# Two transformer blocks on one core: transposes placed inside matmul groups, the projection of p in four pieces, and six slabs of the second input projection by seven block products

## The reference, cut to what matters

```python
# first block, after both mixers
merged = sigmoid(ga) * (y_a @ w_branch_a) + sigmoid(gb) * (y_b @ w_branch_b)
h = h + rms_norm(merged @ w_out, norm_post_mix)
v = rms_norm(h, norm_pre_mlp)
h = h + rms_norm(square(relu(v @ w_up)) @ w_down, norm_post_mlp)
e = (p @ w_ple) * sigmoid(h @ w_ple_gate)      # p: 256 x 256
h = h + rms_norm(e, norm_ple)
# second block
qa, ka, va, qb, kb, vb, qi, ki, wi, ga, gb = split(rms_norm(h, g_mix_2) @ w_in_2)
# rope on qa, ka, qb, kb, qi, ki; two attentions; 32 experts of three matrices each
```

## Time and profile before

| | us |
|---|---|
| median of 3 runs | 1460.21 (1456.59 to 1465.51) |
| the profiled execution's own time | 1465.0 |
| its span, first to last instruction | 1463.2 |
| TensorE busy | 1217.1 (83%) |
| VectorE, ScalarE, GpSimd busy | 396.3, 233.0, 137.6 |
| mean granted TensorE clock | 0.922 of full speed |

### The profile page before, as it was taken

One profiled execution on the slowest core, in us unless ns is written; L12 is line 12 of the kernel. 1 busy time (PEld: TensorE's weight loads), 2 busy tenths in 40 slices (PEclk: granted clock), 3 DMA queues, 4 the chain that ended last, 5 costly groups with the idle time before them and its releaser, 6 DMA issues.

```text
span 1463.2 us, 13835 instructions
## 1 busy us (share of the span) xinstructions
PE 1217.1 (83%) x5929; PEld 687.9 (47%) x5929; DVE 396.3 (27%) x734; ACT 233.0 (16%) x455; POOL 137.6 (9%) x165
## 2 busy tenths in 40 slices
PE   7999999999998999999899999887564664656545
PEld 7846655556844998444444446444221221212211
DVE  2242333035514553644322352213000000000002
ACT  1130003126601221000200165001000000000001
POOL 1001003000210223631112000100000000000000
PEclk9999999999999999999999999997887887868868
DMA  9532222431134344343334210692999999999994
GB/s 370 218 123 112 79 106 110 165 145 58 58 137 153 150 173 173 137 179 157 117 115 173 87 58 29 274 384 110 429 428 429 427 427 428 429 427 427 428 424 186
DMA packets 26980, 330.66 MB, mean 226 GB/s; under 512 B 4112, under 2 KB 4896, under 8 KB 6176
## 3 DMA queue, kind: packets, MB, share of 16 engines
q1 hardware_dynamic: 26912, 329.70, 56.0%
HBM read 328.64 MB, written 1.05 MB: 225 GB/s over the span
## 4 chain that ended last, share of the span: by engine, by line
PE 74%; DMA 15%; DVE 6%; ACT 2%; issue 1%; POOL 0%; SPq 0%; DVEq 0%; ACTq 0%; POOLq 0%
PE ps L226 70%; DMA arena<-in_w 9%; DMA ring<-in_w 4%; PE ps L229 4%; DMA misc<-in_w 2%; DVE arena L293 1%; DVE arena L1508 0%; DVE arena L1503 0%; DVE m L1507 0%; DVE arena L1750 0%; DVE arena L290 0%; DVE arena L1769 0%; ACT arena L1776 0%; ACT arena L288 0%; DMA cols<-in_cols 0%
## 5 line engine op out<-in xcount | busy, mean ns | idle before, releaser
L226 PE MATMUL ps<-ring,arena 128*128 128x512 f32 (+2 forms) x2104 | 777.7, 623 | 114.8 <-DMA arena<-in_w 64.4
L226 PEld LDWEIGHTS ps<-ring,arena 128*128 128x128 f32 (+2 forms) x2104 | 299.1, 166 | 493.6 <-issue 483.7
L226 PE MATMUL ps<-arena 128*128 128x128 f32 (+9 forms) x2268 | 449.2, 418 | 84.7 <-DMA misc<-in_w 32.8
L226 PEld LDWEIGHTS ps<-arena 128*128 128x128 f32 (+3 forms) x2268 | 243.5, 171 | 196.6 <-issue 158.0
L226 PE MATMUL ps<-arena,ring 128*128 128x128 f32 (+1 forms) x768 | 114.3, 310 | 3.6 <-DVE arena L293 2.7
L226 PEld LDWEIGHTS ps<-arena,ring 128*128 128x128 f32 x768 | 106.4, 191 | 10.8 <-issue 2.7
L1769 DVE TENSOR_TENSOR arena<-ps,arena 128x512 f32<-128x512 f32 x8 | 5.5, 692 | 372.2 <-PE ps L226 372.2
L226 PE MATMUL ps<-misc,arena 128*32 128x512 f32 (+3 forms) x232 | 90.1, 549 | 0.0
L229 PE MATMUL ps<-cst,arena 128*128 128x128 f32 x472 | 66.4, 285 | 27.3 <-DVE arena L1740 12.6
L229 PEld LDWEIGHTS ps<-cst,arena 128*128 128x128 f32 x472 | 55.7, 146 | 49.9 <-issue 22.3
L1028 ACT ACTIVATE arena<-arena,nmx 128x128 f32<-128x128 f32 (+1 forms) x96 | 43.6, 454 | 26.4 <-DVE nmx L1026 23.8
(11 more groups left out here) (253 smaller groups left out, 634.3 us busy)
## 6 DMA issues: line engine op xcount, KB each, us to landing
ring<-in_w SPq DMA_DIRECT2D x45, 2048.0 KB, 29.6
arena<-in_w SPq DMA_DIRECT2D x38, 2048.0 KB, 29.8
ring<-in_w_in SPq DMA_DIRECT2D x27, 2048.0 KB, 7.8
misc<-in_w SPq DMA_DIRECT2D x9, 2048.0 KB, 31.8
ring<-in_w_up SPq DMA_DIRECT2D x8, 2048.0 KB, 7.5
ring<-in_w_down SPq DMA_DIRECT2D x8, 2048.0 KB, 7.6
ring<-in_w_out SPq DMA_DIRECT2D x4, 2048.0 KB, 12.2
ring<-in_w SPq DMA_DIRECT2D x5, 1024.0 KB, 21.2
```

Source lines behind the costliest of these rows:

```text
L226: return lambda q: q.matmul(out_, l, r, start=s, stop=e, skip_group_check=skip)
```

## The change

- `pipeline` takes a call that is made between the last two groups of values: the transposes of half 0 of the mixer's output.
- `tile_group` splits a group of eight matmuls in two and calls what stands in `mids` between them. The transposes of a half are put there: half 1 of the mixer's output, both halves of `merged`, half 0 of X after the norm, and so on.
- `norm_add` becomes `norm_half`, called for one half at a time.
- The projection of p becomes four pieces of two matmuls, `ple_part`: two in the first pair of w_up, two between the products of the last two slabs of w_down. Its weights go to `U(7)` instead of the ring, by a load of their own.
- The last pair of w_up gets the first slab of w_down as its next job; its token sums go to the hook after product 6. The order of the last products of w_down changes.
- qi and qa, ka and qb, kb and va are computed in pairs by `seven`; only vb goes by `project`. `seven` has hooks after products 1, 2, 6 and 3, in which transposes, the index projection and rope stand.

The diff, cut to its core:

```diff
+        def tile_group(o, lhs, m, W, nk, mid, *tokens):
+            fns = [mm(o, lhs[:, c, m * 128:m * 128 + 128], W[:, c, :], c == 0, c == nk - 1) for c in range(nk)]
+            if mid is not None:
+                pe.group(fns[:nk // 2], list(tokens))
+                mid()
+                fns = fns[nk // 2:]
+            return pe.group(fns, list(tokens))
...
-        pipeline(jobs, 2)
+        pipeline(jobs, 2, lambda: ybt.append(turn_half(OBN, YBT, None, 0, ob_tok[0], qt_toks)))
...
-        W, tw, k = slab(A["w_ple"], 2)
...
-        for i in range(2):
-            project(W[:, :, i * 512:i * 512 + 512], tw, None, PTT, 2, ptt, lambda P, t, i=i: ev_ple(P, t, i))
...
+        weigh_by_half(lambda i: A["w_branch_b"][i], YBT, 8, ybt, GB, gb_t, GA, mg_t,
+                      {(0, 0): lambda: ybt.append(turn_half(OBN, YBT, None, 1, ob_tok[1], qt_toks)), (0, 1): None, (1, 0): None,
+                       (1, 1): lambda: mtt.append(turn_half(GA, MTT, None, 0, mg_t[0]))})
...
+        part = tiled(0, mtt[0], (None, lambda: mtt.append(turn_half(GA, MTT, None, 1, mg_t[1]))))
+        t_ple = sp.dma(U(7), A["w_ple"], s_ple, 16, pe.now())
         idxw = U(13)[:, 0:576]
+        t_row1 = sp.dma(rowb[1][:, :], A["norm_post_mlp"][0].partition_broadcast(128), s_row1, 16, ptt)
...
         job = next_job([A["w_up"][0], A["w_up"][1]], {n: [att_over, pe_ybt] for n in (4, 5, 6)})
         for op in job["ops"]:
             op()
...
+        t_h1.append(norm_half(0, part, MG, rowb[0], t_small))
...
+        part = tiled(1, mtt[1:], (None, lambda: t_v.append(turn_half(X, XT, cols[:, 8:16], 0, t_h1[0]))))
+        t_h1.append(norm_half(1, part, MG, rowb[0], t_small))
...
         def rest_of_up():
-            t_v.append(turn_half(X, XT, cols[:, 8:16], 1, t_h[1]))
+            t_v.append(turn_half(X, XT, cols[:, 8:16], 1, t_h1[1]))
             sums(t_v[1])
+            P, i = unit()
+            for m in range(2):
+                unit_users[i] = ple_part(m, 0, P[:, m * 512:m * 512 + 512], unit_users[i] if m == 0 else None)
...
-            nxt = next_job([A["w_up"][2 * i + 2], A["w_up"][2 * i + 3]], {}) if i < 3 else None
+            nxt = next_job([A["w_up"][2 * i + 2], A["w_up"][2 * i + 3]], {}) if i < 3 else down_slab(0)
...
+        for s_ in (6, 7):
+            down_products(s_, (1, 2, 6, 5, 3))
...
+        t_sp = ple_part(0, 1, spare)
+        down_products(6, (7, 4))
+        t_h2.append(norm_half(0, y_part(0), YN, rowb[1], t_row1, SC2))
+        t_sp = ple_part(1, 1, spare, t_sp)
...
+        gt_ = [turn_half(X, XT, None, 0, t_h2[0])]
+        down_products(7, (7, 4))
...
+        pairs = [("qi", "qa"), ("ka", "qb"), ("kb", "va")]
+        job = next_job([w_in2[place[n]] for n in pairs[0]], {n: pe.now() for n in (4, 5, 6)}, TB2)
+        for op in job["ops"]:
+            op()
...
+        part = gated(0, gt_[0], (None, lambda: gt_.append(turn_half(X, XT, None, 1, t_h2[1]))))
+        t_h.append(norm_half(0, weighed(0, part), MG, rowb[0], t_row2))
+        part = gated(1, gt_[1], (None, lambda: t_u.append(turn_half(X, XT, cols[:, 16:24], 0, t_h[0]))))
+        t_h.append(norm_half(1, weighed(1, part), MG, rowb[0], t_row2))
...
+            if i == 0:
+                hooks = {1: second_half, 2: after_second, 6: index_rest, 3: lambda: to_rope("qa", 1)}
...
+                hooks = {1: lambda old=old: to_turn(old[1], 1), 2: lambda old=old: to_turn(old[0], 0),
+                         6: turn_ki if i == 1 else None, 3: lambda pair=pair: to_rope(pair[1], 1)}
+            tmp_free = seven(job, S, tmp, tmp_free, False, put, nxt, hooks)
+            to_rope(pair[0], 0)
```

More of the change, by code:

```diff
@@ L1053, in attention, with pipeline @@
             return scores, turned, values, soft
-        def pipeline(jobs, every):
+        def pipeline(jobs, every, late=None):
             n = len(jobs)
@@ L1068, in pipeline @@
                     jobs[x - 3][2]()
+                if x == n + 1 and late is not None:
+                    late()
         OB = U(11).rearrange("p (m h d) -> p m h d", m=2, h=16)
@@ new lines, in build @@
+        t_h2.append(norm_half(1, y_part(1), YN, rowb[1], t_row1, SC2))
+        tap("h2", U(0), t_h2)
+        at["unit"] = ua
+        gated, ii = by_tile(lambda i: A["w_ple_gate"][i], XT)
+        place = {"qa": 0, "ka": 1, "va": 2, "qb": 3, "kb": 4, "vb": 5, "qi": 6}
+        TB2 = [four(U(x)) for x in (7, 8, 11)]
+        pairs = [("qi", "qa"), ("ka", "qb"), ("kb", "va")]
+        job = next_job([w_in2[place[n]] for n in pairs[0]], {n: pe.now() for n in (4, 5, 6)}, TB2)
+        for op in job["ops"]:
+            op()
@@ L1366, in build @@
-        t_h = norm_add(weighed, MG, rowb[0], t_row2, None, begin)
-        done(first["slab"][2], first["qi"])
-        tap("h3", U(0), t_h)
-        t_rs = row_scale(X, SC3, t_h)
-        for m in range(2):
-            for x in (C_C2, C_S2):
-                a = cst[:, x + m * 32:x + m * 32 + 32]
-                t_tab = dve.op(lambda q, a=a, m=m: q.tensor_scalar(a, a, column(SC3 + m), None, ALU.mult), t_rs)
+        t_h = []
+        part = gated(0, gt_[0], (None, lambda: gt_.append(turn_half(X, XT, None, 1, t_h2[1]))))
@@ new lines, in index_part, with second_half @@
+        def index_part(m):
+            return pe.group([mm(PX[:, m * 512:m * 512 + 72], XT[:, c, m * 128:m * 128 + 128], iw3[:, c, :], c == 0, c == 7) for c in range(8)],
+                            t_idx, t_u[m], unit_users[xi] if m == 0 else None)
+        index_part(0)
+        ki = sb("ki", 256)
+        ki3 = ki[:, :].rearrange("p (m n) -> p m n", m=2)
+        wi = sb("wi", 16)
+        wi3 = wi[:, :].rearrange("p (m n) -> p m n", m=2)
+        turned_in = {}
+        def second_half():
+            t_u.append(turn_half(X, XT, cols[:, 16:24], 1, t_h[1]))
+            sums(t_u[1])
@@ new lines, in build, with to_rope, to_turn, turn_ki @@
+        KIT = U(4, 0.125, 1024)
+        STG3 = [v.rearrange("p (m n) -> p m n", m=2) for v in STG]
+        ready = {}
+        stg_free = [[dve.now()], [dve.now()]]
+        def to_rope(n, w):
+            if n not in dstV:
+                ready[n] = rope_full(STG3[w], STG3[w], 8, ready[n])[1]
+        def to_turn(n, w):
+            if n not in dstV:
+                tT[n], t = turn4(n, STG3[w], ready[n])
+                stg_free[w] = [t]
+        def turn_ki():
+            P, i = unit()
+            t = pe.group([tr(P[:, m * 128:m * 128 + 128], ki3[:, m, :]) for m in range(2)], turned_in["ki"], unit_users[i])
+            turned_in["kit"] = unit_users[i] = act.op(lambda q: q.activation(KIT, P[:, 0:256], ACT.Copy), t, t_u)
@@ L1468, in build @@
+        for n in dstV:
+            tV[n] = got.get(n, [])
+        W, tw, k = slab(w_in2[place["vb"]], 8)
+        project(W, tw, k, XT, 8, t_u, scaled_to(dstV["vb"].rearrange("p (m n) -> p m n", m=2), SC3, tV["vb"], pe.now()))
+        to_turn("kb", 0)
+        t_ki, t_wi = turned_in["kit"], turned_in["wi"]
         RL = U(10)
```

356 lines of the change are left out of this document (160 added, 196 removed).

## The result

| | before | after |
|---|---|---|
| median of the runs | 1460.21 us | 1471.43 us (1467.66 to 1473.25, 7 runs) |
| ratio to before, 95% interval | 1 | 1.0076 [1.0051, 1.0101] |
| profiled execution, its span | 1465.0, 1463.2 us | 1471.4, 1469.6 us |
| mean granted clock of it | 0.922 | 0.921 |

The account below looks back on a forecast made before the run. TensorE's list was taken as the path up to the experts' stream; its three stretches summed +10.3 - 3.8 - 0.6 = +5.9 us, profiled execution 1465.0 to 1471, median 1460.2 to 1466; range of 8 in 10: 1453 to 1478.

Parts of the forecast that it names:

- Stretch A, the new wait: Projection of p to w_up's first product: late loads idle TensorE about 23 us, making the stretch 10 us longer.
- the first rival: w_up's loads come in time, so projection of p to w_up gains 15.1 us; 1441 us in all, chance 0.08.
- Stretch B: From w_up's first product to the end of products 1, 2, 6, 5, 3 of w_down's last two slabs: -3.8 us.
- Stretch C: From w_down's last products to the index scores: fewer products, more waits and low clock, -0.6 us in sum.
- The wait ahead of product 1 of ka, qb: Second input projection: TensorE idles 3.9 us because VectorE gets late to L451, 14.2 us of work against 10.3.
- the port: VectorE slowed beside GpSimd's additions in the pairs: 2 us as upper end, none taken in the sum.
- The gate's transposes: Weight sums of qi, qa ahead of the third norm cost nothing; if 1 us longer, TensorE waits 1 us.
- The clock: Before the index scores: 2.5 us of low clock behind each of three waits, 7.5 us.
- The loads in time: Same as the first rival: w_up's loads are not late; 1441 us, chance 0.08.
- VectorE sets the pace of the pairs: Second input projection: wait before ka, qb 10 us, L451 3 us late in both later pairs; 1481 us, chance 0.13.
- The loads share the rate: Before w_up: its next two slabs slow the awaited ones, wait 9.8 us longer; 1476 us, chance 0.09.
- Clock stays high: No 2.5 us of low clock at the four waits; 1456 us, chance 0.12.

Follow-up runs that it names:

- Run 1: The changed kernel with the load of w_ple issued behind the first two slabs of w_up instead of ahead of them: 1449.78 us, ratio to before 0.9909.
- Run 8: The changed kernel with only the sum z+v of the first pair moved from GpSimd to VectorE: 1466.11 us, one execution.
- run 3: The changed kernel with row scale, rope tables, index weights and rope of ki recorded behind product 2, not 6, of pair qi, qa: 1461.10 us.
- run 4: The changed kernel with the second input projection slab by slab in full products, without pairs: 1463.92 us, ratio to before 1.0027.
- run 6: The changed kernel with the edits of run 1 and run 3, and ScalarE squaring before it evicts a piece of p: 1435.26 us.
- run 7: The changed kernel with the edits of run 1 and run 4: 1437.38 us, ratio to before 0.9830.

## Why the prediction was right, and where it was not

The time lies inside the range, on the side and within the 1% that had most of the chance. By its own steps, stretch by stretch, the sum was +5.9 and the traces show +10.95 - 4.9 + 4.1 = +10.15; the medians +11.2. That the profiled execution came out at 1471.4 where the prediction had 1471 is luck: its +6.4 is the +10.15 less 2.8 us by which its attention ended sooner and 1.0 behind the index scores.

**Stretch A, the new wait: as worked out.** w_ple's load was issued at 440.49, and the second slab landed when I had it: 17.4 us by my sum, 457.88 - 440.49 = 17.39 in the trace. The idle is 23.00 against "about 23". The clock behind it cost 3.0 for 2.5 (0.9 on the transposes; 5.53 from 475.50 to 481.03 for eight instructions that take 3.43). +10.95 for +10.3. Run 1 shows the cause, and also the other end of that term: with no wait the stretch is 58.88 + 0.9, 15.2 shorter than before, for the -15.1 of the first rival. The attention ended 2.8 us earlier in after's trace by the clock's luck, so all instants of the prediction were that much late, and the differences not.

**Stretch B: right.** -4.9 for -3.8; the waits at w_down's start and for the token sums are gone. The one microsecond more I did not trace in full; in part it is that a wait costs more than its bracket: from 499.41 to 504.02, 32 instructions that take 3.57 and a wait of 0.88, are 4.61 us.

**Stretch C is the step that failed: +4.1 for -0.6.** The sum of the waits was mis-sized: 12.8 by my count, 17.2 in the trace. The idle of before was right (7.2).
- The wait ahead of product 1 of ka, qb: 7.44 for 3.9. I added up VectorE's list from product 6 on and left out what it waits for. Two things stand in it, in the timelines of VectorE (first and last), ScalarE and GpSimd:

```profile
744.11 2.29 DVE L378 TENSOR_TENSOR arena<-ring,arena 128x2048 f32<-128x2048 f32 x1 [1.11 <-PE ps L226]
747.67 0.15 DVE L275 TENSOR_SCALAR stats<-stats 128x1 f32<-128x1 f32 x1 [1.28 <-ACT junk L273]
```

```profile
746.49 1.06 ACT L273 ACTIVATE junk<-arena 128x1024 f32<-128x1024 f32 x1 [1.86 <-DVE arena L378]
```

```profile
752.91 2.30 POOL L1421 TENSOR_TENSOR ki<-arena 128x64 f32<-128x64 f32 x1 [23.70 <-DVE arena L1420]
755.17 0.32 POOL L1422 TENSOR_TENSOR ki<-arena 128x64 f32<-128x64 f32 x1
755.55 0.29 POOL L1456 COPY ki<-ki 128x128 f32<-128x128 f32 x1
755.80 1.26 POOL L443 TENSOR_TENSOR arena<-arena 128x512 f32<-128x512 f32 x1
```

```profile
752.75 2.28 DVE L381 TENSOR_TENSOR ring<-ring 128x2048 f32<-128x2048 f32 x1
757.10 0.69 DVE L447 TENSOR_TENSOR arena<-arena 128x512 f32<-128x512 f32 x1 [2.07 <-POOL arena L443]
...
760.91 0.68 DVE L451 TENSOR_TENSOR arena<-ps,arena 128x512 f32<-128x512 f32 x1
```

  The squares of the row scale wait for a weight sum (L378, until 746.40) ahead of them and VectorE stands 1.28 us for the squares. And GpSimd's z+v (L443) stands in its list behind the rope of ki, which comes only after VectorE's row scale; the result L447 waits 2.07 us for it. The two make 3.35 of the 3.5 missed. Run 8 took the second away, -1.56; run 3 took both out of this place with the whole index work. The first alone was not tried. Of the 2.07, nearly all is the term that the prediction called the port and put at nothing in its sum, with 2 us as its upper end: the first rope addition (L1421, 752.91) took 2.30 us beside VectorE's weight sum L381 and the next one, of the same size, 0.32. Without these 1.98 us z+v would have ended at 755.08, when VectorE was just done with L381 (755.03); that is an estimate from these rows, and no run separates the two instructions.
- The gate's transposes: 1.00 for nothing. The prediction had named it ("if they are 1 us longer"). No run undid it alone; in run 4, which has no such weight sums there, it is gone. Half of it may be the port again: the first of the four weight sums there (L375, 698.81) took 2.82 us for 2.29, beside a GpSimd addition of 698.51 to 699.47.
- The other waits: 3.51 for 3.4 (run 6 shows its cause: 1.66 with the squares first), 2.81 for 3.7, and 0.88, 0.64, 0.88 for two of 0.9.
- The clock: about 5.2 lost for 7.5 (1.4, 1.4 and 2.4 behind the three long waits). But before had lost only about 4.9 where I had put nearly 7, so by luck the two errors nearly cancel. One price of 2.5 for all these gaps is too coarse: 3.0 and 2.4 were lost behind 23.00 and 7.44, 1.4 behind 3.51 and 2.81, and behind the same wait of 3.5 us the transposes took 1.94 here and 1.06 in runs 3 and 7.

**The rivals.** The loads in time: excluded by the 23.00, and run 1 is that case made real. VectorE sets the pace of the pairs: half of it. The first pair suffered as the rival had it, at 7.44 between 3.9 and 10; the two later pairs wait 0.88, not 3. The loads share the rate: excluded by the landing at 457.88. Clock stays high: excluded, the transposes took 1.94 three times in the rows above.

## What to carry to other kernels

A load that waits for a late event delays every load behind it on its queue, however early those could go: put the one with the late condition last, and only then judge the rest of a change. When you sum an in-order engine's list, walk through every other engine that it waits for and ask what stands ahead in *its* list; here a small sum on GpSimd (2.07 us) and two squares on ScalarE (1.28) stood in a wait of 7.44 that I had put at 3.9. A scheme that saves products at the price of sums and recombinations has to be compared with the plain form at the same place, as it can spend most or all of its gain on waits.
